# Earlier weight splits at entry, later ones for the second query tile, and two residual sums moved from VectorE to GpSimd, in a one-core multi-layer kernel

## The reference, cut to what matters

```python
sh, sc, ga = adaln(cond, w_mod[l], b_mod[l])            # silu(cond) @ w_mod + b_mod, for latent and context
h = rms_norm(x, g_pre[l]) * (1 + sc) + sh               # entry
xv, g_hy, q, k, v, g_att = split(h @ e_w_in)            # 6656 columns
y = concat(hyena(xv) * silu(g_hy), attention(q, k, v) * silu(g_att)) @ e_w_out
x = x + ga * rms_norm(y, g_post[l])                     # residual, for latent and for context
```

## Time and profile before

| | value |
|---|---|
| median of 3 runs | 1976.3 us (1975.82 to 1976.98) |
| profiled execution | 1976.62 us |
| its span, first to last instruction | 1974.8 us |
| mean granted clock of TensorE | 0.976 of full |
| busy: PE, DVE, ACT, POOL | 94%, 57%, 45%, 3% |

### The profile page before, as it was taken

How to read it: one execution, slowest core, us unless ns; L and a number is a source line. 1 busy time by engine, 2 the same in 40 slices (tenths; PEclk the granted TensorE clock), 3 DMA queues, 4 the chain that set the end, 5 groups by cost and what they waited for, 6 DMA issues and landing times. The chain is left out here.

```text
span 1974.8 us, 24150 instructions
## 1 busy us (share of the span) xinstructions
PE 1864.6 (94%) x9290; PEld 1500.5 (76%) x9290; DVE 1118.6 (57%) x1986; ACT 888.0 (45%) x1385; POOL 55.9 (3%) x62
## 2 busy tenths in 40 slices
PE   6999899899989899999997999999999999999997
PEld 3666678777778677777776888779987878779986
DVE  3525165756533845666565666466645667466654
ACT  3313344422133625566553545536634555635542
POOL 1000000000000000000000001000000001000000
PEclk8989999999999999999998999999999999999999
DMA  9315512121123533333234444455555444455552
GB/s 353 128 37 194 186 65 65 43 75 43 65 107 117 171 95 99 107 118 112 98 113 131 150 129 143 158 171 170 181 193 171 145 150 139 149 171 170 176 203 81
DMA packets 113962, 265.12 MB, mean 134 GB/s; under 512 B 4743, under 2 KB 8104, under 8 KB 113784
## 3 DMA queue, kind: packets, MB, share of 16 engines
q1 hardware_dynamic: 109408, 248.47, 38.3%
q0 software_dynamic: 3184, 10.85, 1.6%
q10 hardware_dynamic: 1256, 4.25, 0.5%
HBM read 262.51 MB, written 1.05 MB: 133 GB/s over the span
## 5 line engine op out<-in xcount | busy, mean ns | idle before, releaser
L144 DVE TENSOR_TENSOR qw_rest<-weights,qw_lead 128x1024 fp32r<-128x1024 f32 (+2 forms) x428 | 524.1, 1227 | 505.6 <-ACT qw_lead L315 504.6
L315 ACT ACTIVATE qw_lead<-weights 128x1024 fp32r<-128x1024 f32 (+2 forms) x428 | 448.1, 1048 | 663.2 <-PE psum L153 638.6
L153 PE MATMUL psum<-qw_lead,b_h_lead 128*128 128x512 f32 (+1 forms) x480 | 199.1, 415 | 10.0 <-DVE hT L2802 5.4
L153 PE MATMUL psum<-qw_lead,b_h_rest 128*128 128x512 f32 (+1 forms) x480 | 187.9, 391 | 0.0
L153 PE MATMUL psum<-qw_rest,b_h_lead 128*128 128x512 f32 (+1 forms) x480 | 187.7, 391 | 0.0
L153 PE MATMUL psum<-e_h_lead,qw_lead 128*128 128x512 f32 x320 | 144.8, 453 | 6.3 <-PEq L118 5.7
L153 PE MATMUL psum<-b_h_lead,qw_lead 128*128 128x256 f32 x512 | 145.7, 285 | 0.0
L153 PE MATMUL psum<-b_h_rest,qw_lead 128*128 128x256 f32 x512 | 145.3, 284 | 0.0
L153 PE MATMUL psum<-b_h_lead,qw_rest 128*128 128x256 f32 x512 | 145.3, 284 | 0.0
L153 PE MATMUL psum<-e_h_lead,qw_rest 128*128 128x512 f32 x320 | 127.0, 397 | 0.0
L153 PE MATMUL psum<-e_h_rest,qw_lead 128*128 128x512 f32 x320 | 126.3, 395 | 0.0
(11 more groups left out here) (463 smaller groups left out, 3518.4 us busy)
## 6 DMA issues: line engine op xcount, KB each, us to landing
weights<-in_w_in SPq DMA_DIRECT2D x48, 1024.0 KB, 5.1
weights<-in_o_w_in SPq DMA_DIRECT2D x32, 1024.0 KB, 5.3
weights<-in_w_mlp_up SPq DMA_DIRECT2D x32, 1024.0 KB, 5.4
weights<-in_w_mlp_down SPq DMA_DIRECT2D x32, 1024.0 KB, 4.8
weights<-in_e_w_in SPq DMA_DIRECT2D x26, 1024.0 KB, 5.2
weights<-in_w_mod SPq DMA_DIRECT2D x24, 1024.0 KB, 6.1
weights<-in_e_w_out SPq DMA_DIRECT2D x8, 1024.0 KB, 4.9
weights<-in_o_w_out SPq DMA_DIRECT2D x8, 1024.0 KB, 4.9
```

Source lines behind the costliest of these rows:

```text
L144: return eng.tensor_tensor(self.rest[at], src, self.lead[at].bitcast(F32), ALU.subtract)
L153: mm = nc.tensor.matmul(out, l, r, start=start and i == 0, stop=stop and i == 2)
L315: self.core.nc.scalar.activation(self.buf.lead[self.at(u)], self.raw(u), ACT.Copy).then_inc(self.lead_ready, 1)
```

## The change

Three edits, each in the even layer. The first two units' splits at entry go from places -1.9 and -1.2 to -2.95 and -2.9 (ACT leads -2.93 and -2.88, DVE rests -2.65 and -2.6). The shift of the splits that begins at `e_q2` goes from 0.35 to 1.75 places. The two residual adds of the context tiles go from DVE to POOL, from places 34.7 and 34.9 to 32.1 and 32.4, and ACT's squares of those tiles from 35.0 and 35.3 to 34.4 and 34.8. Nothing else changes; the sums are the same.

```diff
-    def __init__(self, core, tag, dense, tiles, gate_of, st, junk, tmp, places, x_in=None):
+    def __init__(self, core, tag, dense, tiles, gate_of, st, junk, tmp, places, x_in=None, by_pool=()):
...
+        self.by_pool = by_pool
...
-        self.vector, self.scalar = (self.means, self.products, self.adds), (self.squares, self.roots)
+        self.vector, self.scalar, self.gpsimd = (self.means, self.products, self.adds), (self.squares, self.roots), (self.pool_adds,)
...
         for t in range(self.tiles):
+            if t in self.by_pool:
+                continue
             yield self.places[t][3]
...
+    def pool_adds(self, pool):
+        core, nc = self.core, self.core.nc
+        for t in self.by_pool:
+            yield self.places[t][3]
+            if self.x_in:
+                self.x_in(pool)
+            pool.wait_ge(self.read, t + 1)
+            nc.gpsimd.tensor_tensor(core.x[:, t, :], core.x[:, t, :], self.tmp[t % 2], ALU.add).then_inc(self.x_ready, 1)
...
-    run_stages(core, [dense, enter, filt, mods0, mods1, rotary, head_turn, Feed(core, (dense,), (mods0, mods1), prime=(-1.9, -1.2, 3.0), late=(first["e_q2"], 0.35), floor=(first["e_kv"], 3.1)),
+    run_stages(core, [dense, enter, filt, mods0, mods1, rotary, head_turn, Feed(core, (dense,), (mods0, mods1), prime=(-2.95, -2.9, 3.0), late=(first["e_q2"], 1.75), floor=(first["e_kv"], 3.1)),
...
-                   [(29.6, 29.7, 29.9, 30.1), (29.8, 30.0, 30.3, 30.4), (31.5, 31.8, 32.0, 34.7), (31.9, 32.2, 32.3, 34.9)], x_in=lambda dve: dve.wait_ge(x_in, 32))
+                   [(29.6, 29.7, 29.9, 30.1), (29.8, 30.0, 30.3, 30.4), (31.5, 31.8, 32.0, 32.1), (31.9, 32.2, 32.3, 32.4)], x_in=lambda eng: eng.wait_ge(x_in, 32), by_pool=(2, 3))
...
-                   st[:, 16:32], [(30.6, 30.8, 30.9), (30.9, 31.2, 31.3), (35.0, 35.2, 35.6), (35.3, 35.5, 35.8)], ((32.5, 0.15), (38.4, 0.3)))
+                   st[:, 16:32], [(30.6, 30.8, 30.9), (30.9, 31.2, 31.3), (34.4, 35.2, 35.6), (34.8, 35.5, 35.8)], ((32.5, 0.15), (38.4, 0.3)))
```

## The result

| | before | after |
|---|---|---|
| median of 4 runs | 1976.06 us (1975.11 to 1976.98) | 1964.07 us (1961.25 to 1964.96) |
| ratio of the times | | 0.9937, interval 0.992 to 0.9954 |
| profiled execution, its span | 1976.62 us, 1974.8 | 1963.42 us, 1961.6 |
| mean granted clock | 0.976 | 0.980 |

A forecast was written before the change was run, and what follows sets the result against it. PE is busy nearly everywhere, so only its waits and half-clock stretches can give time. The terms -4.3 - 6.1 + 0 = -10.4 us take the median of 1976.3 to about 1966, range 1958.5 to 1972.5.

The forecast's parts named there:

- case (a): Whole kernel: the forecast itself holds, a time of 1961.5 to 1969 us; chance 0.55.
- Edit 1, -4.3: Entry: half 8 lands before PE asks and the clock falls later; -4.3 us, bounds 0 and -6.6.
- Edit 2, -6.1: Second tile's end -2.0, gates -5.0, phase's end +0.9; together -6.1 us, bounds -8 and -4.
- gates' -5.0: Gates: PE's 3.19 us wait before 210.44 goes, with the half clock that follows; -5.0 us.
- second tile's end -2.0: Second tile's end: the head copy PE waited 1.37 us for is ready, some shorter waits go; -2.0 us.
- They end over 1.2 us (one rest) sooner: Second tile's end: DVE's output copies, no longer behind a waiting lead, end over 1.2 us sooner.
- no DMA wait of a lead between 175 and 215: Second tile and gates: sign that the shift of 1.75 works, no lead waiting for DMA from 175 to 215.
- Edit 3, 0: Residual adds: -3.6 us gained and +3.3 of DVE standing nearly cancel; 0, bounds -4.2 and +2.5.
- Rival (c): Residual adds: POOL's adds cost DVE nothing; -4.2 us more, 1962, with the clock held at entry 1959; chance 0.12.
- (b): Entry: the late row copy is paid, half 8 lands near 46; 1970 us, up to 1972.5; chance 0.21.
- (d): Second tile and gates: ACT idle at new places too, or leads wait elsewhere; -2 us, 1970; chance 0.06.
- (e): Units of `e_q2` and `e_gatt`: splits too late for PE, 8 units wait about 2 us each; 1988, chance 0.02.

The follow-up runs named there:

- edit 2 alone: Only the shift of splits from `e_q2` on, 0.35 to 1.75, on the kernel before: 1969.45 us against 1976.53, ratio 0.9967.
- shift 1.05: The changed kernel with a shift of 1.05 instead of 1.75: 1963.49 us against 1975.56 for the kernel before, ratio 0.9942.
- edit 1 alone: Only the entry's splits moved, to -2.95 and -2.9, on the kernel before: 1972.76 us against 1976.53, ratio 0.998.

## Why the prediction was right, point by point

**The sum.** Forecast -10.4, measured -12 (-9 to -16); case (a). The change's second set of runs stood at 1965.45, half a microsecond from the predicted 1966.

**Edit 1, -4.3: measured -4.0 alone (-2.2 to -5.7), -3.9 to -4.4 by the places.** Right: the copy at 26 (25.96), POOL at 26.9 (26.84), half 8's landing at 42 to 43.5 (43.3, and 43.8 and 44.1 in two further executions), the last sum without a wait, x turns at 58 (57.41). That the late start and the early issue are needed together is shown by the two kernels that had one each. Mis-sized inside: the last sum ran at 45.2, not 44.15. PE's early half clock lasted 10.24 us in this execution (27.2 to 37.4), 6.83 before, and the first split matmul came at 31.36 and not 30.9; in the other four executions with early splits the third sum came at 42.89 to 43.63, about where I had put it (43.1). On the other side the clock fell at 51.1, not 48.6, and for 3.41 us, where I had counted 14 matmuls at half rate, 6 us; in two of the five executions it did not fall there at all. The two misses nearly cancel, so that the x turns came within 0.6 us of 58 is in part luck.

**Edit 2, -6.1: measured -6.5 alone (-4.0 to -9.1), -6.2 in the trace.** The gates' -5.0 is 4.97, the phase's end +0.9 is 0.82, the second tile's end -2.0 is 2.04. The step "They end over 1.2 us (one rest) sooner" was put at the wrong lead in part: 1.2 of the 2.0 belong to place 24.37, where the rest held up the sums of squares and not the output copies. And the sign I gave for it, "no DMA wait of a lead between 175 and 215", is wrong: ACT stands 4.47 at 184.93. A wait of an engine costs what is queued behind it, not its length. This was the better half of my own argument, and I should have named the queue and not the wait as the sign.

**Edit 3, 0: trace -0.7 to -1.0, alone -2.4 (0.2 to 4.5).** The two terms nearly cancel as said: 3.3 us of standing were forecast, 2.7 came, because POOL's adds take 2.35 and not 2.55 and only the second stands in a split's way in full. PE's wait of 4.07 was to fall to about 1 and fell to 0.60, and the half clock behind the new idle stretch (put at +1.5) came, but in place of the one at 670. Rival (c), free adds, falls by the stretched cast and split, and by the kernel without POOL that is as fast. The Trainium skill (SBUF — State Buffer, "SBUF: two separate sides") says that GpSimd and VectorE share one pair of SBUF ports, and that whichever starts first holds it for its whole instruction while the other blocks; on VectorE's side this concerns instructions with two SBUF inputs or in a two-port mode. The trace agrees for the split with its two SBUF inputs (2.45) and for the multiply that reads psum, which the rule leaves free (1.28). The cast has one input and was held up too (0.94); that it runs in a two-port mode no run here shows.

**Rivals (b), (d) and (e)** all fell: half 8 landed in time, edit 2 alone gave over three times the 2 us of (d), and no unit was late.

## What to carry to other kernels

Where an in-order engine waits for a transfer, ask what that PE needs is queued behind the wait, and move the waiting step behind just that; half of the shift had all of the gain here. Here a transfer came sooner only when it was issued before its queue ran dry and the rival queue started later: either alone bought nothing that could be measured. Two adds moved to GpSimd beside VectorE's splits cost VectorE more time here (2.7 us standing) than doing them there (2.35).

## What was not expected of the hardware

With half 8 issued at 31.6 into a nearly dry queue beside a busy q0, q1 moved 5 packets from 34 to 36 and 49 from 36 to 37, while with the half issued ahead of the dry moment it moved 115 from 34 to 36. What holds the first packets was not tried. Where both queues have work they move nearly the same number of packets (117 and 115 in the change from 34 to 36, 119 and 119 before from 32 to 34); q0's are of about 4 KB and q1's of 2, and q0 has 65% of the engines' time in both windows.

The record of the granted clock is not complete. In the kernel with shift 1.05, PE runs 6 split matmuls in 2 us from 32 to 34, the rate that the earlier trace rows show at half clock, and the record says 1.00; with edit 1 alone they follow each other at 0.43 us from 32.4 to 34.1 under a record of 1.00. The length of the matmuls is the surer sign.

And executions of one entry differ mostly by the clock: the old entry's x turns lie between 57.63 and 62.29, the new one's between 56.12 and 57.41, so taking away PE's wait also took away most of the spread.
